# Three normalizations of a fused fp32 block: the matmul jobs beside them taken one token tile at a time

## What is computed

```
x = x + gt_a * (mix_in @ w_o)                            # 2048x2048
h = rmsnorm(x, norm_ffn) * (1 + sc_f) + sh_f             # first boundary
gate, up = split(h @ w_gate_up)                          # 2048 x 2*5632
x = x + gt_f * ((silu(gate) * up) @ w_down)              # 5632x2048
x = rmsnorm(x, final_norm)                               # second boundary,
h = rmsnorm(x, a_norm_2)                                 # two norms in a row
u, v, g = split(h @ a_w_in_2)                            # 2048 x 3*4096
y = gelu(u) * spatial(rmsnorm(gelu(v), a_v_gain_2))
x = x + (y * silu(g)) @ a_w_out_2                        # 4096x2048
out = rmsnorm(x, final_norm_2)                           # the end
```

## Time and profile before

| | |
|---|---|
| median of 3 runs | 2348.71 us (2347.66 to 2349.70) |
| profiled execution | 2349.77 us, its span 2348.3 us |
| PE busy | 2268.8 us, 97% |
| DVE, ACT busy | 1510.2 us (64%), 1010.1 us (43%) |
| mean granted TensorE clock | 0.988 of full speed |
| read from HBM | 500.41 MB, 214 GB/s over the span |

### The profile page before, as it was taken

The page is one execution under the profiler, slowest core; times in us unless marked ns, Lnnn a source line. Parts: engine busy times, 40 slices in busy tenths (PEclk is TensorE's granted clock), DMA queues, the critical chain, the costliest instruction groups (busy, mean ns, idle before and its releaser), DMA issues.

```text
span 2348.3 us, 27129 instructions
## 1 busy us (share of the span) xinstructions
PE 2268.8 (97%) x10867; PEld 1871.4 (80%) x10867; DVE 1510.2 (64%) x1897; ACT 1010.1 (43%) x1258; POOL 19.3 (1%) x25
## 2 busy tenths in 40 slices
PE   5999999999999989999999999998999999999997
PEld 3678898788888868888888888886888888888886
DVE  5878888878768777655554455466555555555555
ACT  4345444333444444443344434445444444444343
POOL 0000000000000000000000000000000000000000
PEclk9999999999999989999999999998999999999999
DMA  9966747665887768765555555554655555555553
GB/s 362 379 221 211 230 162 254 216 209 180 283 295 273 256 228 287 262 226 181 196 182 194 187 190 182 195 179 163 204 195 187 185 190 194 184 188 193 190 193 109
DMA packets 276156, 504.64 MB, mean 215 GB/s; under 512 B 24000, under 2 KB 38080, under 8 KB 275264
## 3 DMA queue, kind: packets, MB, share of 16 engines
q1 hardware_dynamic: 276032, 502.93, 63.4%
HBM read 500.41 MB, written 2.49 MB: 214 GB/s over the span
## 4 chain that ended last, share of the span: by engine, by line
PE 83%; DVE 8%; DMA 3%; issue 2%; ACT 2%; SPq 1%; POOL 0%; DVEq 0%; ACTq 0%
PE bank L1078 25%; PE bank L1080 25%; PE bank L1079 25%; DVE WL L1782 2%; PE bank L1276 1%; PE bank L1000 1%; DVE GA L1765 1%; DMA A<-in_w_ada_dram 1%; PE bank L1090 1%; PE bank L1092 1%; PE bank L1091 1%; DVE A L1996 1%; ACT WH L1363 1%; PE bank L1248 1%; DMA A<-in_w_in_dram 1%
## 5 line engine op out<-in xcount | busy, mean ns | idle before, releaser
L1782 DVE TENSOR_TENSOR WL<-RAW,WH 128x1024 fp32r<-128x1024 f32 (+1 forms) x728 | 881.9, 1218 | 640.4 <-ACT WH L1363 636.4
L1363 ACT CAST WH<-RAW 128x1024 fp32r<-128x1024 f32 (+1 forms) x728 | 757.5, 1046 | 899.7 <-PE bank L1080 724.1
L1078 PE MATMUL bank<-WH,HTh 128*128 128x512 f32 x1984 | 792.9, 400 | 10.5 <-DVE WL L1782 5.5
L1080 PE MATMUL bank<-WH,HTl 128*128 128x512 f32 x1984 | 776.9, 392 | 0.0
L1079 PE MATMUL bank<-WL,HTh 128*128 128x512 f32 x1984 | 776.6, 391 | 0.0
L1078 PEld LDWEIGHTS bank<-WH,HTh 128*128 128x128 f32 x1984 | 375.0, 189 | 94.0 <-issue 10.7
L1079 PEld LDWEIGHTS bank<-WL,HTh 128*128 128x128 f32 x1984 | 375.5, 189 | 80.1 <-issue 4.8
L1080 PEld LDWEIGHTS bank<-WH,HTl 128*128 128x128 f32 x1984 | 374.8, 189 | 79.6
L1765 DVE SCALAR_TENSOR_TENSOR GA<-RAW,ST,GA 128x512 f32<-128x512 f32 x264 | 181.1, 745 | 17.4 <-DMA RAW<-in_w_ada_dram 12.2
L1078 PE MATMUL bank<-WH,R2h 128*128 128x512 f32 x408 | 163.7, 401 | 5.6 <-DVE R2l L2106 3.0
L1080 PE MATMUL bank<-WH,R2l 128*128 128x512 f32 x408 | 159.8, 392 | 0.0
(11 more groups left out here) (254 smaller groups left out, 1669.4 us busy)
## 6 DMA issues: line engine op xcount, KB each, us to landing
RAW<-in_a_w_in_dram SPq DMA_DIRECT2D x96, 1024.0 KB, 5.1
RAW<-in_w_gate_up_dram SPq DMA_DIRECT2D x88, 1024.0 KB, 5.0
RAW<-in_w_ada_dram SPq DMA_DIRECT2D x80, 1024.0 KB, 5.5
RAW<-in_w_in_dram SPq DMA_DIRECT2D x63, 1024.0 KB, 5.0
RAW<-in_w_down_dram SPq DMA_DIRECT2D x44, 1024.0 KB, 5.0
RAW<-in_a_w_out_dram SPq DMA_DIRECT2D x32, 1024.0 KB, 5.0
A<-in_w_ada_dram SPq DMA_DIRECT2D x16, 1024.0 KB, 12.0
RAW<-in_w_o_dram SPq DMA_DIRECT2D x16, 1024.0 KB, 5.1
```

Of the source, the lines that this page charges most:

```text
L1078: e.matmul(o, ah[:, s], hi[:, k, :], start=first, stop=False)
L1080: i = e.matmul(o, al[:, s], hi[:, k, :], start=False, stop=last)
L1363: e.copy(hi, rv).then_inc(S["hi"], 1)
L1782: e.tensor_tensor(lo, rv, hi.bitcast(F32), ALU.subtract).then_inc(S["lo"], 1)
```

## The change

Five jobs beside the three norms no longer run both tiles side by side. `run_blocks` runs tile 0 over a block of halves and then tile 1 over the same, kept, halves: 8 halves for the last `wo` job and the first `gate` job, 6 for the last `down` job and (6, 1, 1) for the first `v2` job, 4 for the last `wout` job. The additional places lie over buffers that are free then (`EXTRA_A`, `EXTRA_R`). `done_tile` handles a tile as soon as its own pass is over (new semaphore `tile`). Each token tile then has its own chain: residual, square, factor; `turn_n` scales x by the factor while tokens are still on partitions, half of the width on DVE and half on ACT; `turn_t` transposes the scaled rows, four blocks to a bank; `turn_g`, four per tile, applies column scale and shift with four 128x128 activations from PSUM, then rounds 512 columns at once (ACT), and DVE subtracts 512 at once. The broadcast by matmul is gone. No `w_ada` load of the last group stands among the loads of the last `wo` and first `gate` job. At the end each tile is scaled by DVE (1280 columns) and ACT (768) together and stored by itself; the product with `final_norm_2` moves behind the square. The constant -0.5 for POOL comes from the constants instead of a memset.

```diff
+EXTRA_A, EXTRA_R = (4, 5, 6, 7), (8, 9)
...
+    last_wo, last_down, last_wout = d1[3], ffn[-1], g2[-1]
+    last_wo.blocks, last_wo.extra, last_wo.early = (8,), EXTRA_A, 1
+    ffn[0].blocks, ffn[0].extra = (8,), EXTRA_A
+    last_down.blocks, last_down.extra, last_down.early = (6,), EXTRA_R, 2
+    g2[0].blocks, g2[0].extra = (6, 1, 1), EXTRA_R
+    last_wout.blocks, last_wout.early = (4,), 3
...
+        self.places = [(self.WH[:, n, :], self.WL[:, n, :]) for n in range(NHL)]
+        self.places += [(self.over(f"WHx{n}", 24 + 8 * n, 1024, FR), self.over(f"WLx{n}", 28 + 8 * n, 1024, FR)) for n in range(4)]
+        self.places += [tuple(f[:, 1024 * n:1024 * n + 1024] for f in flat) for n in range(2)]
...
-                if extra and k % 2 == 0:
+                if extra and k % 2 == 0 and (extra[0][1] < 20 or (j.name, j.c) not in (("wo", 3), ("gate", 0))):
...
+        place = self.free_place(j)
+        self.place.append(place)
+        self.after.append(self.user[place] + 1)
+        self.user[place] = hid
...
+    def free_place(self, j):
+        n = min(tuple(range(NHL)) + j.extra, key=lambda n: self.user[n])
+        return n if self.user[n] < self.used else None
...
+    def run_blocks(self, j):
...
+        first, steps = self.used, 2 * self.total
+        for n, size in enumerate(j.blocks):
+            for tt in range(2):
+                for hid in range(first, first + size):
+                    self.fill(2)
+                    while len(self.halves) <= hid:
+                        self.stage_next()
+                    hj, t0, nk = self.halves[hid][:3]
+                    assert hj is j
+                    for k in range(nk):
+                        self.settle(self.need(j, t0 + k, tt))
+                    self.put("half", hid, pr, tt)
+                    self.used += tt
+                    steps -= 1
+                    self.left = (steps + 1) // 2
...
+                        if j.early:
+                            self.done_tile(j, pr, tt)
+                        elif tt:
+                            self.retire(j, pr)
...
+    def done_tile(self, j, pr, tt):
+        t, r, c = {"wo": (2, 0, j.c), "down": (3, 3, 3), "wout": (5, 7, 3)}[j.name]
+        if tt == 0:
...
+        self.put("res", r, c, pr, tt)
+        self.bg.append(self.turn_last(t, tt))
...
+    def turn_last(self, n, bb):
+        self.put("turn_sq", n, 3, (bb,))
+        yield
...
+        if n == 3:
+            self.ms()
+        self.put("turn_rs", n, bb, self.ms())
+        m = self.ms_n
+        yield
+        yield
+        self.put("turn_n", n, bb, m - (n == 3))
+        for _ in range(3 if n == 2 else 2):
+            yield
+        for g in range(6):
+            if g < 4:
+                self.put("turn_t", n, bb, g)
+            if g > 1:
+                self.put("turn_g", n, bb, g - 2)
+                self.have |= {("h2" if n == 2 else "h3", 4 * g - 8 + k, bb) for k in range(4)}
+            if g % 2:
                 yield
...
-            self.put("turn_t", n, c, g)
-            yield
-    def turn_tiles(self, n, prefix):
-        self.marks[("ht_free", n)] = self.used
-        self.put("turn_b", n)
-        for g in range(9):
-            self.put("turn_g", n, g)
-            if g:
...
+        for j in J["d"][:-1]:
             self.run(j)
-        self.settle(("gta", 3))
...
+        self.run_blocks(J["d"][-1])
+        self.turn_bg = []
+        self.run_blocks(J["ffn"][0])
+        for j in J["ffn"][1:-1]:
+            self.run(j)
+        self.run_blocks(J["ffn"][-1])
+        self.turn_bg = []
+        self.run_blocks(J["gmlp"][0])
+        for j in J["gmlp"][1:-1]:
+            self.run(j)
+        self.run_blocks(J["gmlp"][-1])
...
-            i.then_inc(S["half"], 1)
+            if tiles[-1] == 1:
+                i.then_inc(S["half"], 1)
+            elif t0 + nk == j.nkt and j.early:
+                i.then_inc(S["tile"], 1)
...
-            for q in range(4):
-                kt, bb = 4 * c + 2 * g + q // 2, q % 2
-                i = e.transpose(bank[n][:, q * P:(q + 1) * P], L.X[:, bb, kt * P:(kt + 1) * P], ident)
-            i.then_inc(S["turn_t"], 1)
...
+            t, bb, g = args
+            tile = 2 * (t - 2) + bb
+            W.wait_ge("turn_d" if g < 2 else "turn_x", 2 * tile + g % 2 + 1)
+            take(4 + g)
+            src = L.XS if t == 2 else L.X
+            four(bank[4 + g], [src[:, bb, (4 * g + q) * P:(4 * g + q + 1) * P] for q in range(4)]).then_inc(S["turn_t"], 1)
+            held[4 + g] = [(f"t{t}_m", 16 * bb + 4 * g + 4)]
...
-            W.wait_ge("half", hid - NHL + 1)
+            W.wait_ge("half", sch.after[hid])
+            if sch.place[hid] >= NHL:
+                W.wait_ge(*extra_free(sch, sch.place[hid]))
...
+        elif kind == "turn_n":
+            t, bb, m = args
+            W.wait_ge("rsq", m)
+            W.wait_ge("turn_t", 8 * (t - 2))
+            for c in (2, 3):
+                cs = slice(512 * c, 512 * c + 512)
+                if t == 2:
+                    e.activation(L.XS[:, bb, cs], L.X[:, bb, cs], ACT.Copy, scale=L.turn_rs[2][:, bb:bb + 1]
+                                 ).then_inc(S["turn_x"], 1)
+                else:
...
+                    e.activation(L.X[:, bb, cs], L.XS[:, bb, cs], ACT.Copy, scale=L.turn_rr[:, bb:bb + 1]
+                                 ).then_inc(S["turn_x"], 1)
...
+        elif kind == "turn_g":
+            t, bb, g = args
+            i, ts = 4 * bb + g, slice(bb * P, (bb + 1) * P)
+            tm = L.TM[i % 2].rearrange("p (k t) -> p k t", t=P)
+            W.wait_ge("turn_t", 8 * (t - 2) + i + 1)
+            W.wait_ge(f"t{t}_lo", i - 1)
...
+            for q in range(4):
+                kt, b = 4 * g + q, bank[4 + g][:, q * P:(q + 1) * P]
+                if t == 2:
+                    e.activation(tm[:, q, :], b, ACT.Identity, scale=L.cAf[:, kt:kt + 1], bias=L.cBf[:, kt:kt + 1]
+                                 ).then_inc(S["t2_m"], 1)
                 else:
-                    W.wait_ge("mod", mod_value(CHUNK_OF[48 + 4 * (g // 2)]))
-                    for q in range(2):
-                        e.activation(L.HTh[:, 2 * g + q, :], tm[:, q, :], ACT.Identity,
-                                     bias=L.cBf[:, 2 * g + q:2 * g + q + 1]).then_inc(S["t2_hi"], 1)
+                    e.activation(tm[:, q, :], b, ACT.Copy, scale=L.colAN[:, kt:kt + 1]).then_inc(S["t3_m"], 1)
+            W.wait_ge(*tile_free(sch, t, bb))
+            W.wait_ge(f"t{t}_m", 4 * i + 4)
+            e.copy(L.HTh[:, 4 * g:4 * g + 4, ts], tm).then_inc(S[f"t{t}_hi"], 1)
...
+def tile_free(sch, t, bb):
+    return ("half", job_end(sch, *(("wo", 3) if t == 2 else ("down", (2, 3))))) if bb else ("tile", t - 1)
...
+            t, bb = args[:2]
+            m, one = L.turn_m[t][:, bb:bb + 1], slice(bb, bb + 1)
+            W.wait_ge(f"t{t}_sq", 14 + 2 * bb if t == 3 else 7 + bb)
...
+        elif kind == "turn_n":
+            t, bb, m = args
+            W.wait_ge("rsq", m)
+            W.wait_ge("turn_t", 8 * (t - 2))
+            for c in (0, 1):
+                cs = slice(512 * c, 512 * c + 512)
+                if t == 2:
+                    e.tensor_scalar(L.XS[:, bb, cs], L.X[:, bb, cs], L.turn_rs[2][:, bb:bb + 1], None, ALU.mult
+                                    ).then_inc(S["turn_d"], 1)
...
         elif kind == "turn_g":
-            t, g = args
-            ops = 2 if t == 2 else 1
...
-                W.wait_ge(f"t{t}_lo", ops * (g - 1))
-                e.tensor_tensor(L.TM[g % 2].rearrange("p (k t) -> p k t", t=T), L.XT[:, 2 * g:2 * g + 2, :], rb, ALU.mult
-                                ).then_inc(S[f"t{t}_m"], 1)
...
+            t, bb, g = args
+            i, ts = 4 * bb + g, slice(bb * P, (bb + 1) * P)
+            W.wait_ge(*tile_free(sch, t, bb))
+            W.wait_ge(f"t{t}_hi", i + 1)
+            e.tensor_tensor(L.HTl[:, 4 * g:4 * g + 4, ts], L.TM[i % 2].rearrange("p (k t) -> p k t", t=P),
+                            L.HTh[:, 4 * g:4 * g + 4, ts].bitcast(F32), ALU.subtract).then_inc(S[f"t{t}_lo"], 1)
...
-            m, = args
+            bb, m = args
             W.wait_ge("rsq", m)
-            W.wait_ge("t5_f", 8)
-            for h in range(2):
-                hs = slice(1024 * h, 1024 * h + 1024)
-                e.tensor_scalar(L.X[:, 0, hs], L.X[:, 0, hs], L.turn_rs[5][:, 0:1], None, ALU.mult).then_inc(S["out_d"], 1)
+            W.wait_ge("t5_f", 7 + bb)
+            e.tensor_scalar(L.X[:, bb, 0:1280], L.X[:, bb, 0:1280], L.turn_rs[5][:, bb:bb + 1], None, ALU.mult
+                            ).then_inc(S["out_d"], 1)
...
+            bb, _ = args
+            for name, hs in (("out_d", slice(0, 1280)), ("out_a", slice(1280, 2048))):
+                W.wait_ge(name, bb + 1)
+                e.dma_start(out[bb * P:(bb + 1) * P, hs], X[:, bb, hs]).then_inc(S["out"], 16)
+            if bb:
+                W.wait_ge("out", 64)
```

(23 more changed lines are left out.)

263 lines of the change are left out of this document (106 added, 157 removed).

## The result

| | before | after |
|---|---|---|
| median | 2349.20 us (4 runs beside the change) | 2322.88 us (2322.74 to 2324.40) |
| profiled execution, its span | 2349.77, 2348.3 | 2322.96, 2321.7 |
| mean granted TensorE clock | 0.988 | 0.994 |

The ratio is 0.9889, 95% interval [0.9872, 0.9906]: 26 us faster, inside the forecast range of 2316 to 2338, 3 us under the forecast of 2326. The direction and the size are as predicted. So the total is near in part by luck.

A forecast was written before the change was run, and what follows sets the result against it. PE bounds the kernel, so time comes only from its gaps at three norms: 3.8 (end) + 11.1 (first boundary) + 7.7 (second) = 22.6 us off, median 2326 us, range 2316 to 2338.

The forecast's parts named there:

- Tile 0 covered, one wait for tile 1: First boundary: PE starts `gate` with no wait for tile 0, then waits 3.3 us before tile 1's transposes.
- The waits: PE idle: first boundary 3.3 us before tile 1's transposes; second 0.4 before tile 0's, 2.4 before `v2`, 2.8 before tile 1's.
- Edits at nothing: keeping halves: First passes: keeping weight halves costs nothing, as four `wo` halves lie ready and gate's follow at 1.36 us each.
- second boundary: `down` to `v2`: 14.2 us lost before, 5.6 of waits and 0.9 of transposes remain, 7.7 us gained.
- rival C: First passes: weight splits set the pace, +0.8 us for each of 32 halves, 26 us, 2352 us; chance 0.04.
- Both signs by which the prediction was to be wrong: PE's timeline: first-pass matmuls waiting for weight residuals (L1883), or matmul intervals of 0.43 us following the idle spells.
- rival A: At three waits of 2.4 to 3.3 us PE's clock falls, 2.3 us each: +6.9, 2333 us; chance 0.2.
- The sum: All three norms: 3.8 + 11.1 + 7.7 = 22.6 us off the profiled 2349.8; median 2326 us.
- first boundary: `wo` to `gate`: 15.3 us lost before becomes 3.3 of wait plus 0.9 of transposes, 11.1 us gained.
- tail: End of the kernel, after the last matmuls: 11.9 us becomes 8.1, 3.8 us saved, bounds 2.5 to 5.2.
- under "nothing": POOL's constant instead of the memset: lies 15 us ahead of its first use, so no cost or gain.
- Rivals B and D: B: boundary waits close, 2317 us, chance 0.15. D: ACT too far behind, boundary gaps stay whole, 2345 us, chance 0.06.

The follow-up runs named there:

- the split put forward: The changed kernel with one more weight split put ahead of the residual and squares of the job before each pass job; 2323.44 us, ratio 0.9885.
- the second trace of after: The changed kernel itself, unaltered, run and traced once more; 2325.88 us, ratio 0.9897.
- the 32-byte run: The changed kernel with its arena moved up by 32 bytes; 2331.23 us, ratio to the kernel before 0.9922.

## Why the prediction was right, and where its steps failed

**Tile 0 covered, one wait for tile 1.** Right at both boundaries, place by place. The run without passes shows that the passes are what covers it.

**The waits.** 3.3, 2.4, 2.8 and 0.4 us were forecast; 1.96, 2.48, 1.46 and 0.3 were measured, 6.2 for 8.9. ACT's groups were right: the four activations of a group take 1.52 us until their rounding starts (841.16 to 842.68 in after's trace), where I took 4 x 0.37 = 1.48 from the rows. The Trainium skill ("ScalarE: Activation LUTs", "What ACT_TABLE_LOAD costs") led to 4 x 0.39, by an estimate; the trace lies between.

**"Edits at nothing: keeping halves."** This step failed. A first pass takes a half in 1.36 us instead of 2.7, so the second half of the job is wanted 1.4 us earlier, and at that moment ACT and DVE are busy with the job before: at the second boundary with its residuals and four squares, at the first with its residuals and two squares. Hence the late residuals of 1.06 and 2.30 us, which the split put forward removed. That is rival C's mechanism, at two halves instead of 32. The 0.89 us before L1102 is the same crowd seen from the other side. Both signs by which the prediction was to be wrong, waits for L1883 in the first passes and intervals of 0.43 us behind a spell, are in the traces; what they cost is small beside what the passes give.

**The clock** (rival A). I took it as held for spells up to 3.3 us. It does not go by the spell's length alone: 1.96 us lowered it in after, 1.97 at the same place with the arena 32 bytes up did not; 2.30 at 1571.90 did not, 2.38 at the same place in the second trace of after did. The Trainium skill ("TensorE: Matmul & The Clock Gate", "HAM oscillation") warns that idle gaps of PE throw the clock back to half; the spells of 1.96 and 2.38 us agree with that, those of 1.97 and 2.30 us do not. A fall behind one of these spells cost 1.6 us, not 2.3 (from L1069 at 847.59 to the next one 3.92 us, with the clock held 2.32 at the same place of the 32-byte run; 1.6 too at 1574.92 in the second trace of after); the one at 821 us in the second trace of after, behind a spell of 0.94 us, cost about 2.5.

**The sum.** With the arena at a multiple of 128 bytes in both, before against the two traces of after: first boundary 7.1 and 5.0 us (forecast 11.1), second 6.9 and 5.8 (forecast 7.7), tail 4.0 less 0.5 for the last job's passes (forecast 3.8). That is 17.4 and 14.3 against 22.6. The medians say much the same: with the arena off a multiple of 128 in both, the change gains 18.3 and 19.0 us (ratios 0.9922 and 0.9919, 3.5 us to either side). The first boundary is the term that was mis-sized: 1.2 us of late residual, 1.0 before L1102 and 1.6 of clock are the parts that the rows of after's first trace show; the wait before L1069 gives 1.3 back (1.96 for 3.3), so some 1.5 of the 4.0 us are not located. Of the rest of the total, 5.8 us in the stages came from the arena; the first trace's total also holds 2.8 us ahead of the first cut, where no job is changed. The constant was in the prediction under "nothing", with its own cost rightly nothing; what it moved was not looked at.

**Rivals B and D** did not come; C came in small, A in part.

## What to carry to other kernels

Two tiles that share weights can cover each other's norm if one runs a whole pass ahead, but the pass takes weights twice as fast: look at which split stands behind the retiring of the job before. When a change alters the size of any buffer, see where the ones behind it now start, and run that shift alone. Compare traces stage by stage between the same operations: here the stage without a norm repeats to 0.1 us, one with a norm to 1 or 2, and a median does not tell 3. So trace the same kernel twice before reading a small difference in a stage.
